# The high part of W copied by ScalarE, with VectorE making the low part of U in between

## What is computed

```python
s = einsum('nhpd,hpkd->nhpk', q, peer_keys)         # scores of 8 heads, 2 x 128 keys
...
e = take_along_axis(cand_idx, g_i, axis=-1)         # 16 experts of each head
g = softmax(g_s, axis=-1)
act = gelu(einsum('nd,nhkd->nhk', xb, peer_u[e]))
return einsum('nhk,nhkd->nd', (g * act), peer_v[e])
```

## Time and profile before

| | us |
|---|---|
| time, median of 3 runs | 3191.28 (3190.05 to 3193.43) |
| span of the profiled execution, which is the time of its own that the page gives | 3195.1 |
| PE busy | 2866.6 (90%) |
| PE weight loads busy | 2291.1 (72%) |
| DVE busy | 1910.5 (60%) |
| ACT busy | 1048.6 (33%) |
| POOL busy | 384.6 (12%) |

### The profile page before, as it was taken

One profiled execution on the slowest core, in us unless ns is written; L12 is line 12 of the kernel. 1 busy time (PEld: TensorE's weight loads), 2 busy tenths in 40 slices (PEclk: granted clock), 3 DMA queues, 4 the chain that ended last, 5 costly groups with the idle time before them and its releaser, 6 DMA issues. The chain is left out here.

```text
span 3195.1 us, 47076 instructions
## 1 busy us (share of the span) xinstructions
PE 2866.6 (90%) x15273; PEld 2291.1 (72%) x15273; DVE 1910.5 (60%) x3793; ACT 1048.6 (33%) x1485; POOL 384.6 (12%) x487
## 2 busy tenths in 40 slices
PE   7979988876898795378999999999999999999997
PEld 3434535555744495357999999999888888888886
DVE  1348736463012368897998888887555555555554
ACT  1112330011202221354445555554333333333332
POOL 0010134101000131360002122221000000000000
PEclk9976795556797697689999999999999999999998
DMA  3000023213220120125666566666555445554543
GB/s 151 10 15 1 15 82 107 76 53 105 107 118 7 42 64 17 69 121 207 209 217 211 203 236 211 238 214 211 189 173 172 163 167 169 170 173 163 175 169 117
DMA packets 206678, 424.82 MB, mean 133 GB/s; under 512 B 20449, under 2 KB 129378, under 8 KB 203618
## 3 DMA queue, kind: packets, MB, share of 16 engines
q1 hardware_dynamic: 191170, 371.23, 34.4%
q0 software_dynamic: 10784, 47.99, 3.9%
q10 hardware_dynamic: 4608, 4.20, 0.4%
HBM read 381.61 MB, written 41.74 MB: 132 GB/s over the span
## 5 line engine op out<-in xcount | busy, mean ns | idle before, releaser
L1929 PE MATMUL psC<-xh,Uh 128*128 128x256 f32 (+1 forms) x2048 | 608.2, 297 | 0.0
L1929 PE MATMUL psC<-xl,Uh 128*128 128x256 f32 (+1 forms) x2048 | 604.3, 295 | 0.0
L1929 PE MATMUL psC<-xh,Ul 128*128 128x256 f32 (+1 forms) x2048 | 603.4, 295 | 0.0
L1948 PE MATMUL psC<-Vh,Wh 128*128 128x512 f32 x1280 | 502.9, 393 | 14.4 <-DVE Wl L1870 9.7
L1948 PE MATMUL psC<-Vl,Wh 128*128 128x512 f32 (+1 forms) x1280 | 502.6, 393 | 0.0
L1827 DVE TENSOR_TENSOR Vl<-rV,Vh 128x1024 fp32r<-128x1024 f32 x256 | 320.1, 1250 | 232.3 <-ACT Vh L1770 232.3
L1770 ACT ACTIVATE Vh<-rV 128x1024 fp32r<-128x1024 f32 x256 | 271.4, 1060 | 413.7 <-PE psC L1948 413.3
L1948 PE MATMUL psC<-Vh,Wl 128*128 128x512 f32 x1024 | 402.2, 393 | 0.0
L1929 PEld LDWEIGHTS psC<-xh,Uh 128*128 128x128 f32 x2048 | 385.4, 188 | 15.1
L1929 PEld LDWEIGHTS psC<-xh,Ul 128*128 128x128 f32 x2048 | 385.4, 188 | 8.8
L1929 PEld LDWEIGHTS psC<-xl,Uh 128*128 128x128 f32 x2048 | 385.3, 188 | 0.0
(11 more groups left out here) (279 smaller groups left out, 3739.5 us busy)
## 6 DMA issues: line engine op xcount, KB each, us to landing
rU<-in_peer_uT SPq DMA_DIRECT2D x256, 512.0 KB, 4.4
rV<-in_peer_v SPq DMA_DIRECT2D x256, 512.0 KB, 3.5
gates<-gst POOLq DMA_DIRECT2D x18, 2048.0 KB, 7.4
gr<-gates SPq DMA_DIRECT2D x32, 640.0 KB, 6.0
arena<-in_poolM SPq DMA_DIRECT2D x128, 128.0 KB, 2.1
gr<-gates SPq DMA_DIRECT2D x32, 512.0 KB, 5.5
wraw<-in_w_pq SPq DMA_DIRECT2D x16, 512.0 KB, 3.3
arena<-in_w_in SPq DMA_DIRECT2D x8, 884.0 KB, 15.9
```

The source lines that it names most:

```text
L1929: last = M(bank(6 + k, hi - lo), a[:, k, c], x[:, d, lo:hi], start=(d == 0 and a is Uh and x is xh), stop=(d == KD - 1 and x is xl))
L1948: last = M(bank(2 * b + n, p1=m), w[:, k, b * P:b * P + m], v[:, k, c], start=(first and a == 0), stop=(final and a == len(parts) - 1), sk ...
```

## The change

The copy of `wf` into Wh goes from DVE to ACT, behind `high_u` and ahead of `high_v`. On DVE `low_u` moves ahead of the low part of W. The waits go with the instructions: ACT now waits for `w_mul` of the same step and for `v_mm` of two steps before, and DVE for `w_hi` from ACT.

```diff
                     A(ge[:, 0:NG], bank(6 + k % 2, NG), ACT.Gelu).then_inc(S["ge_done"], 1)
                     if not (end and k >= 2):
                         high_u(s + 2, k % 2)
+                    act.wait_ge(S["w_mul"], s + 1)
+                    if not known_below(s, 2):
+                        act.wait_ge(S["v_mm"], s - 1)
+                    A(Wh[:, k % 2, 0:NG], wf[:, 0:NG], ACT.Copy).then_inc(S["w_hi"], 1)
                     if not (end and k == 3):
                         high_v(s + 1, 1 - k % 2)
...
                         .then_inc(S["w_mul"], 1)
-                    dve.wait_ge(S["w_mul"], s + 1)
-                    if not known_below(s, 2):
-                        dve.wait_ge(S["v_mm"], s - 1)
-                    V.tensor_copy(Wh[:, k % 2, 0:NG], wf[:, 0:NG]).then_inc(S["w_hi"], 1)
+                    if not (end and k >= 2):
+                        low_u(s + 2, k % 2)
                     dve.wait_ge(S["w_hi"], s + 1)
                     low = V.tensor_tensor(Wl[:, k % 2, :], wf[:, 0:2 * P], Wh[:, k % 2, 0:2 * P].bitcast(F32),
                                           ALU.subtract)
...
                     low.then_inc(S["w_done"], 1)
-                    if not (end and k >= 2):
-                        low_u(s + 2, k % 2)
                     if not (end and k == 3):
                         low_v(s + 1, 1 - k % 2)
```

## The result

The changed kernel takes 3203.36 us, the median of 20 runs (3188.70 to 3210.93); the kernel before, run beside it on the same chip, 3192.36 us, also of 20 runs (3181.92 to 3204.67). The ratio is 1.0032, 95% interval 1.0019 to 1.0044, or 6 to 14 us: slower. The forecast, 3197.4 us and slower by 0.19%, had the direction and lies at the lower end of that interval; the median lies 0.9 us above the range.

A forecast was written before the change was run, and what follows sets the result against it. PE, busy 90%, was taken as the bound, with some 15 us of waits in the dense steps. Terms 2.7 - 0.7 + 1.5 + 2.6 = 6.1 us, on the median 3191.28, gave 3197.4 us; range 3193 to 3202.5.

The forecast's parts named there:

- A: Start of the first group: W's low part waits behind U's late-loaded low part, so PE starts down later, +2.7 us.
- B: Steps with the choice of experts: PE's lag swallows some waits for DVE, -0.7 us, between -2.6 and 0.
- no visible loss: Rival: DVE's relief removes PE's choice-step waits and one-hot quads lose nothing, +2.7 us, 3194.0 us; chance 0.18.
- C: One-hot quads: U's low part meets GpSimd's product, delaying W's low part 0.1 us in each of 18 quads, +1.5 us.
- the longer 0.84: Upper case in the one-hot quads: U's low part waits 0.84 us, losing 0.21 in all 18, 3.8 us.
- D: Start of the second group: late gates and U's load behind them delay W's two low pieces, +2.6 us.
- E: The 124 steady steps: they lose 0.8 of 4.9 us of slack, so no time is lost.
- The clearly slower one: Rival: in one-hot quads products delay both U's and W's low parts, 13 us over 18 quads, 3210 us; chance 0.10.

The follow-up runs named there:

- the gates early: Last gates stored about six steps earlier, against the kernel before: 3180.56 us, ratio 0.9972; the same with the changed order: 3192.65 us, ratio 1.0010.
- cut kernels: Attention stage replaced by loading rows of x, five runs each: old order 2122.74 us, changed 2128.63; with last gates stored earlier, 2115.57 and 2121.80.
- the second comparison: The same two kernels timed again, no edit: before 3196.68 us, ratio 1.0004; changed 3203.85 us, ratio 1.0018, beside 35 runs of before, median 3195.94.
- The order alone: Against the kernel before, only U's low part moved ahead of W's low part, the copy staying on DVE: 3207.56 us, ratio 1.0055.

## Why the prediction was right in kind and too low

*A, the start of the first group:* +2.7 forecast; from 1.27 to 3.98 us, +2.71, and 2.71 to 2.74 in every pair of old and new order in the table. What varies is the landing of the gates: W starts 12.48 to 14.97 us after the first up in the fourteen profiles. That moves a single profile by up to 2.5 us, whatever the change does. PE's wait grew from 8.08 to 10.65 us.

*B, the choice steps:* -0.7 forecast, within -2.6 to 0; measured -0.2 by the means of five profiles each (207.94 and 207.70), which is less than either five scatter by, so its size is not resolved. The lag did swallow waits: behind the first down PE waits for W's low part for 1.0 to 2.4 us in the five profiles of the old order, 1.7 in the mean, and for 0.4 to 1.1, 0.7 in the mean, in those of the new one. Part of that is lost again in the first step, from down(0) to down(1), which takes 7.5 us in the mean before (7.08 to 8.27) and 8.0 with the change (7.53 to 8.45). DVE's 11 us less of work bought nothing, as the text said against the rival of no visible loss.

*C, the one-hot quads:* +1.5 forecast; +2.0 in all three pairs. The mechanism held: U's low part took the copy's place behind the product, and it ended where the forecast put it. The forecast took the copy's wait of 0.73 us from the copy's start, 0.45 us behind W's own start at 1928.50; U's low part starts 0.34 behind that of W (1929.50) and waits 0.84. The two cancel, because the wait ends with the product and not after a fixed time, so the 0.21 for "the longer 0.84" was no bound that could come about here. The price and the count were off in opposite directions: 0.18 and not 0.1 where PE waits, since the weight load can no longer run ahead, and in 10 of the 18 quads, not all. That 1.5 lies so near 2.0 is in part luck.
The Trainium skill, SBUF — State Buffer, "SBUF: two separate sides", which the prediction weighed, states that the loser of the shared port pair fully blocks for the whole instruction. By that rule U's low part of step 77 would have waited 0.98 us, from 1929.84 to the end of the product's row at 1930.82, and the prediction put C at 4.1 us by it. The trace agrees but for the last 0.14 us. A later step of the changed kernel shows a short wait:

```profile
2186.42 1.16 POOL L1720 TENSOR_TENSOR ohC<-ohJ,cT 128x512 f32<-128x512 f32 x1 [17.39 <-DVE ohI L1842]
2186.97 1.70 DVE L1826 TENSOR_TENSOR Ul<-rU,Uh 128x1024 fp32r<-128x1024 f32 x1 [0.29 <-ACT Uh L1764]
```

Taking as the wait what a row is longer than its plain length, the wait of 0.48 ends at 2187.45 and the product's row at 2187.58. The same holds in all rows of DVE from step 36 to 123 that are over 0.3 us longer than plain, 77 before and 74 after: waits from 0.47 to 0.85 us, each ending 0.13 to 0.14 ahead of the end of the product's row. The 0.73 and 0.84 that the prediction set against the rule are shorter than the product because DVE's row starts after the product's.

*D, the start of the second group:* +2.6 forecast; from 1.71 to 4.31 us, +2.60. With the gates early it goes, which shows that it hung on the pairing of late gates and a load behind them.

*E, the steady steps:* nothing forecast; 893.14 us in all fourteen profiles.

The sum by these terms is 2.7 - 0.2 + 2.0 + 2.6 = 7.1 where I had 6.1; the profiles' dense steps give 6.7 (1740.21 less 1733.51), 7.8 (1741.91 less 1734.13) and 7.9 (1741.79 less 1733.92, without attention), the cut kernels 5.9 by medians. Within what can be resolved, the cost was sized right, a microsecond low.

**The step that failed is the last**, from the sum to the time and its range: "on the median the forecast is 3197.4 us", with bounds of +1.7 to +10.1 that came from the four terms alone. The scatter of the base was put at nothing. The base of 3191.28 was the median of three runs within 3.4 us, and I took that closeness for the scatter of the kernel. In sets of 20 to 35 runs the kernel before spreads over 23 to 26 us, in a set of nine over 34, and its median is 3192.36, 3195.94, 3189.32 and 3188.72 in the four sets. Of the 6.0 us between 3197.4 and the measured 3203.36, 1.1 is the base, 1.0 the terms, and 3.9 is in no dense step and in no cut kernel. A median of 20 runs on each side still leaves 4 us of uncertainty either way, so 7.1 is inside what the 20 runs show. The runs' granted clocks point to where most of the 3.9 goes. Over the 47 runs of before and the 12 of the changed kernel on the chip of the second comparison, the time falls by 2.0 us for each 0.001 of mean granted clock, and at equal clock the changed kernel is 5.2 us longer (95% interval 3.5 to 6.9); for the two kernels with early gates it is 5.1 (3.1 to 7.1), where their medians stand 12.1 apart. These two lean low, since the change's own longer waits lower the mean (0.9652 to 0.9634 in the kernels without attention). So the longer times come with lower clocks. That the 3.9 of the first comparison goes the same way is argued, since the clocks of its runs of before are not on record, and whether the change makes runs at a lower clock more frequent is not shown. A base uncertain by some 3 us had to be added to the range; what hinted at it was the stage ahead, with its granted clock of 0.68 and 0.70.

Of the rivals, no visible loss (3194.0) is out: it wanted -2.6 us in the choice steps and nothing in the one-hot quads, and they came to -0.2 and +2.0. The clearly slower one (3210, both low pieces hit in a quad) did not come about: behind U's low part W's low part took its plain 0.4 us in 87 of the 88 steps from 36 to 123. The order alone on DVE loses 7.2 us in the same quads, but not in that way: there the copy meets the product (1.0 us or more instead of 0.3 in 33 steps), and U's low part, plain in 85 of the 88 steps, stands behind it.

## What to carry to other kernels

Before work is moved off a busy engine, ask what the instruction that is waited for last will stand behind in the new order: here W's low part was put behind one that hangs on another load, and 83 us of relief for DVE bought a loss of 6 to 8 us at PE, while storing the gates earlier, which changes no engine's work, gained as much. Price such a change on intervals between rows inside one trace (W to down) and not on whole runs, when a stage ahead of it scatters by more; where the whole must be known, cut that stage away and time what is left. And where a stage runs at a lowered clock, do not take the closeness of three runs for the scatter of the kernel.

## What the hardware showed that was not expected

- The dense steps, behind the same code in every whole kernel, start anywhere within 20 us (1431.70 to 1452.06); without the attention stage they start within 1.6 us (370.25 to 371.87). Of the ten whole profiles, the four that start by 1441.55 had a mean granted clock of 0.79 from 240 to 380 us, the six that start at 1445.20 or later 0.69 or 0.70. In the 20 runs of the changed kernel the two shortest, 3188.70 and 3189.71 us, had a mean clock of 0.895 over the whole run, the two longest, 3210.82 and 3210.93, 0.885 and 0.886. What decides which course a run takes was not tried.
- Once past its start, the dense stage repeats to the hundredth: 893.14 us from down(130) to down(255) in fourteen profiles, at a clock of 1.00, and 562.71 us for the one-hot quads in all three profiles of the old order of gates and steps.
- A copy to fp32r on ACT costs 414 ns for 256 columns and 463 ns for 320. The Trainium skill (ScalarE: Activation LUTs, What ACT_TABLE_LOAD costs) gives 186 ns and 0.833 ns a column for an ACTIVATE with immediate scale and bias, by estimate 399 and 453 ns. The trace agrees within 4%.
